# Expert weights of a hybrid block: loads of 1 MB into twelve slots become loads of 2 MB into six pairs of slots

## The chip, the cores and the metric

The kernel runs on one core of one Trainium2 chip. The metric is the device time of one execution in microseconds (us); before the change it was 2168.43 us, the median of three runs from 2166.55 to 2171.65.

## What is computed

One layer of a block over 512 tokens of width 1024, all in float32. Three token mixers (differential attention, mLSTM, cross-attention to 256 memory tokens) are computed side by side, gated, mixed and added to the input. Then follows the sparse part, which this case is about:

```
h = h + mix @ w_out
n = rms_norm(h)
top_v, top_i = top_k(n @ router_w + router_b, 4)          # 4 of 32 experts for each token
g, u = split(n @ w_gate_up[e] + b_gate_up[e])             # 1024 -> 2 x 1024
a = (clip(u, -7, 7) + 1) * min(g, 7) * sigmoid(1.702 * min(g, 7))
h = h + sum over the 4 experts of share * (a @ w_down[e] + b_down[e])
```

Each expert has 1024 x 2048 weights up and 1024 x 1024 down, 12 MB. All 32 are used, so 384 MB of weights pass through the core once.

## The kernel before

The program runs the mixers first, then the mix and the router, and near 1076 us the expert stage begins (`stage_moe`, from line 2178). The experts are taken in an order of their token counts that the router works out; every other one is "small" (at most 64 tokens).

The 12 MB of an expert are cut into 12 units of 1 MB: 128 partitions by 2048 floats, so that a partition's row of a unit is 8 KB. Units 0 to 3 and 8 to 11 are gate and up weights, units 4 to 7 (`DOWN`) the down weights. Each unit number has one slot in SBUF, `moe_raw[pos]`, at a place where an earlier stage kept something else. Four pairs of neighbouring slots lie in `xnH`/`xnL` (0 to 3) and `mixH`/`mixT` (4 to 7), the others in `y_caT` (8, 9) and `yH` (10, 11). Each slot has its own semaphore `s_moew[pos]`.

A unit goes through four engines. SyncE loads it (`load`, line 2233). ScalarE rounds it to its high part in `moe_hi`, a ring of six tiles (`hi`, line 2238). VectorE subtracts the high part from the raw one and leaves the low part in the slot itself (`lo`, line 2254). TensorE multiplies with both (`unit`, line 2262), 12 products of 128x512 for an ordinary expert, 8 for a small one, and counts the unit as used in `s_use`. ScalarE's rounding of a unit comes five units ahead of TensorE and waits for the unit's load and for the high tile that TensorE gave back six units earlier. VectorE is four units ahead.

TensorE's order in the loop is units 0 to 3 of expert n, units 4 to 7 of expert n-1, then units 8 to 11 of expert n, with the transposes of activations between. At the end (`LAST`) the down units of the last expert come in the order 6, 7, 4, 5. SyncE's list in the expert stage (`refill`, line 2525) is in order of position: wait until the slot's unit has been used, then load the same position of the next expert. After position 3 of the first expert it waits for the residual h with the down bias added, and stores h to the output (line 2535, 2 MB); ScalarE (line 2690) and GpSimd wait for this store before they go on to the second expert, since results are added onto the output in memory.

GpSimd gathers each expert's token rows from memory by an indirect DMA (`fetch`, line 2481) and scatters its results onto the output (`late`, line 2505); the first gather is issued in the router stage (line 1990). Before the expert stage, SyncE loads units 0 to 3 of the first expert early (line 1728) and, when the output projection is done, units 8 to 11 and 4 to 7 (line 1736). A barrier stands between the router stage and the expert stage (line 136).

Of the kernel before, what the change touches and what calls it, by code (L numbers as in the profile page):

```python
# [1601 lines left out]
def stage_mix(K, ctx):  # L1602
# [93 lines left out]
    def _(sp):  # L1696
# [24 lines left out]
        for dst, name in ((braw[0:NE, :], "b_gu"), (braw[NE:2 * NE, :], "b_gu"), (gf[:], "g_ffn"), (rw[:], "rw"),  # L1721
# [4 lines left out]
            sp.dma_start(dst, A[name]).then_inc(s_c, 16)  # L1726
        for u in range(4):
            sp.dma_start(K.moe_raw[u][:], A["w_moe"][u]).then_inc(K.s_moew[u], 16)
        sp.dma_start(K.lists.rearrange("(p r) f -> p (r f)", p=P), A["fill"]).then_inc(K.s_fill, 16)
        sp.dma_start(K.over, A["ove"]).then_inc(K.s_fill, 16)  # L1730
        for t in range(TT):
            sp.wait_ge(s_hn, t + 1)
            sp.dma_start(K.hn_d[t * P:(t + 1) * P, :], hn[:, t, :]).then_inc(s_hd, 16)
        for u in (8, 9, 10, 11, 4, 5, 6, 7):
            sp.wait_ge(s_o, 2 * TT)
            sp.dma_start(K.moe_raw[u][:], A["w_moe"][u]).then_inc(K.s_moew[u], 16)

# [153 lines left out]
    def _(act):  # L1891
# [57 lines left out]
        def moe_hi(u):  # L1949
            act.wait_ge(K.s_moew[u], 16)  # L1950
            act.wait_ge(s_o, TT)
            nc.scalar.activation(K.moe_hi[u][:], K.moe_raw[u][:], ACT.Copy).then_inc(s_mhi, 1)
# [226 lines left out]
def stage_moe(K, ctx):  # L2179
# [3 lines left out]
    HF, U = FF // 2, 4 * (FF // 2)  # L2183
    RAW, LO, HI, s_w, s_LG, s_Xg = K.moe_raw, K.moe_lo, K.moe_hi, K.s_moew, K.s_LG, K.s_Xg
    b0, b1 = K.base[K.xcT.name] + 4 * 2 * U, K.base[K.yH.name] + 4 * KT * S
# [47 lines left out]
    def load(sp, e, pos):  # L2233

        sp.dma_start(RAW[pos][:], A["w_moe"][ds(e * 12 + pos, 1)].rearrange("o p n -> (o p) n")
                     ).then_inc(s_w[pos], 16)

    def hi(act, n, pos):

        if not exists(n, pos):  # L2240
            return
        act.wait_ge(s_w[pos], n * 16 if pos in DOWN else n * 16 + 16)
        if isinstance(n, int) and n == 0:
            if pos in (10, 11):
                act.wait_ge(s_use, count(0, pos - 8))
        elif isinstance(n, int) and n == 1 and pos in (2, 3):
            act.wait_ge(s_use, count(0, pos + 8))
        elif isinstance(n, int) and n == NE:
            act.wait_ge(s_use, count(n - 1, pos if pos >= 6 else pos + 6))
        else:  # L2250
            act.wait_ge(s_use, count(n, pos - 6) if pos >= 6 else count(n - 1, pos + 6))
        nc.scalar.activation(HI[ring(n, pos)][:], RAW[pos][:], ACT.Copy).then_inc(s_hi, 1)  # L2252
# [269 lines left out]
    with nc.Block(no_gpsimd_drain=True) as block:  # L2522
        @block.sync
        def _(sp):
            def refill(n, first=False):

                here, ahead = None if first else expert(sp, n), expert(sp, n + 1)
                for pos in range(12):
                    if first and pos in DOWN:
                        continue  # L2530
                    sp.wait_ge(s_use, count(n, pos))
                    load(sp, here if pos in DOWN else ahead, pos)
                    if first and pos == 3:
                        sp.wait_ge(s_h1, 2 * TT)
                        sp.dma_start(A["out"].rearrange("(t p) d -> p t d", p=P), h1).then_inc(K.s_acc, 16)

            refill(0, True)
            with sp.Fori(1, NE - 1) as n:
                refill(n)
            here = expert(sp, NE - 1)  # L2540
            for pos in DOWN:
                sp.wait_ge(s_use, count(NE - 1, pos))
                load(sp, here, pos)

            def item(i, n):
                e = sp.value_load(K.over_sb[0:1, ds(i * 2, 1)], min_val=0, max_val=NE - 1)
                sp.wait_ge(s_use, i * 12 + B)
                for pos in ORDER:
                    load(sp, e, pos)
            overflow(sp, item, lambda: sp.wait_ge(K.s_ov, 20 * 16))  # L2550
            sp.wait_ge(s_sc, 16 * NE)
# [83 lines left out]
        def _(act):  # L2635
# [72 lines left out]
            def item(i, n):  # L2708
                base = i * 12 + B

                def item_hi(q):
                    pos = ORDER[q]
                    act.wait_ge(s_w[pos], n * 16 + 16)
                    act.wait_ge(s_use, base + (q - 5 if q >= 6 else 0))
# [147 lines left out]
def program(nc, A):  # L2862
    with ExitStack() as ctx:
# [17 lines left out]
        with ExitStack() as c0:  # L2881
# [9 lines left out]
            with ExitStack() as c1:  # L2891
                K.memH, K.memL = (K.sb(n, [P, KT, M], R32, ctx=c1) for n in ("memH", "memL"))
                with ExitStack() as c2:
# [28 lines left out]
                    [K.base[K.y_caT.name] + 4 * U * j for j in range(2)] + [K.base[K.yH.name] + 4 * U * j for j in range(2)]  # L2922
            K.moe_raw = [K.place(f"moe_raw{j}", U, at) for j, at in enumerate(homes)]
            K.moe_lo = [K.rounded(f"moe_lo{j}", K.moe_raw[j]) for j in range(12)]
            homes = [K.base[wraw.name] + 4 * U * j for j in range(4)] + [K.base[K.xcT.name] + 4 * U * j for j in range(2)]
            K.moe_hi = [K.place(f"moe_hi{j}", U, at, R32) for j, at in enumerate(homes)]
            K.moe_Xg = K.place("moe_Xg", D, K.base[K.sg[0].name])
            K.s_moew = [nc.alloc_semaphore(f"moe_unit{j}") for j in range(12)]
            K.s_acc, K.s_fill, K.s_ov, K.s_LG, K.s_Xg = (nc.alloc_semaphore(n) for n in (
# [7 lines left out]
def layouts(x, mem, attn_norm_g, w_in, b_gate, da_q_norm_g, da_k_norm_g, da_lambda_q1, da_lambda_k1,  # L2937
# [88 lines left out]
    for i, w in enumerate(units):  # L3026
        moe[:, i] = w.transpose(0, 1, 3, 2, 4)
    out["w_moe"] = moe.reshape(NE * 12, P, 4 * HF)
    out["b_gu"] = np.asarray(b_gate_up)[0].reshape(NE, 2, 2, HF).transpose(0, 2, 1, 3).reshape(NE, 2 * FF)
# [22 lines left out]
```

## Time and profile before

| | |
|---|---|
| median of three runs | 2168.43 us |
| profiled execution: span from first to last instruction | 2168.4 us (the profile gives no other time of its own) |
| TensorE products busy | 2111.0 us, 97% of the span |
| VectorE busy | 1564.6 us, 72% |
| ScalarE busy | 1318.4 us, 61% |
| GpSimd busy | 566.5 us, 26% |
| expert weight loads | 384 of 1024 KB, median 8.4 us from issue to landing |
| memory traffic in the expert stage | 383 to 405 GB/s in the profile's slices |

TensorE's busy time is an average over stages, and a busy TensorE is not one at its peak. In the slices of the expert stage TensorE, VectorE and the DMA engines all read nine tenths or more, so their shares alone do not say which of them sets the pace; the waits do. The rows further below are of the views that show them.

### The profile page before, as it was taken

The numbers are of one execution on the slowest core, as the hardware profiler recorded it, in microseconds if no ns is written. First come the engines' busy times: TensorE is split into PE (matmuls) and PEld (weight loads), VectorE is DVE, ScalarE is ACT, GpSimd is POOL, SyncE is SP. The second block draws the span as 40 slices with busy tenths as digits, with TensorE's granted clock in tenths as the row PEclk, the third lists the DMA queues.
The fourth block names the chain that finished last, engine by engine and source line by source line (L and its number), as shares of the span: only waits on it lengthen the run. The fifth ranks groups of instructions, "written<-read, shape, count | busy, mean of one in ns | idle before, by whom it ended". The sixth has DMA issues, their size and how long they took to land.

```text
span 2168.4 us, 29886 instructions
## 1 busy us (share of the span) xinstructions
PE 2111.0 (97%) x9638; PEld 1652.6 (76%) x9638; DVE 1564.6 (72%) x1690; ACT 1318.4 (61%) x1606; POOL 566.5 (26%) x429
## 2 busy tenths in 40 slices
PE   6999899999999999999899999999999999999998
PEld 6888677776667888888767777777777777777776
DVE  6777454754444334434689999999999999999996
ACT  5566453334232433323468888888888888888884
POOL 3333100201232000000214234443244332343421
PEclk9999999999999999999799999999999999999999
DMA  5110232320112343435589999999999999999993
GB/s 193 59 58 29 98 117 78 133 78 30 49 40 88 97 136 97 136 96 165 204 325 376 405 391 391 405 391 401 392 391 399 397 385 402 388 393 399 393 395 120
DMA packets 87095, 516.01 MB, mean 238 GB/s; under 512 B 13124, under 2 KB 14148, under 8 KB 36264
## 3 DMA queue, kind: packets, MB, share of 16 engines
q1 hardware_dynamic: 79448, 498.30, 59.6%
q0 software_dynamic: 7296, 16.79, 3.2%
q8 instruction: 37, 0.61, 0.1%
q14 instruction: 26, 0.21, 0.0%
q10 hardware_dynamic: 288, 0.09, 0.0%
HBM read 504.91 MB, written 19.40 MB: 242 GB/s over the span
## 4 chain that ended last, share of the span: by engine, by line
PE 49%; DVE 1%; DMA 0%; ACT 0%; issue 0%; POOL 0%; POOLq 0%; DVEq 0%; ACTq 0%
PE bank L2276 9%; PE bank L2278 8%; PE bank L2277 8%; PE bank L2269 8%; PE bank L2270 8%; PE bank L2311 3%; PE bank L2298 1%; PE bank L2287 1%; PE bank L2360 1%; DVE moe_lo L2259 1%; DMA out<-y_daT 0%; PE bank L2347 0%; DVE y_daT L2336 0%; ACT moe_hi L2252 0%; PE bank L2352 0%
## 5 line engine op out<-in xcount | busy, mean ns | idle before, releaser
L2259 DVE TENSOR_TENSOR moe_lo<-moe_raw,moe_hi 128x2048 fp32r<-128x2048 f32 x382 | 857.1, 2286 | 7.1 <-ACT moe_hi L2252 5.4
L2252 ACT ACTIVATE moe_hi<-moe_raw 128x2048 fp32r<-128x2048 f32 x380 | 722.3, 1915 | 62.8 <-PE bank L2278 54.4
L173 ACT ACTIVATE unit_hi<-unit_raw 128x1024 fp32r<-128x1024 f32 x116 | 122.2, 1059 | 241.8 <-DMA unit_raw<-in_w_units 235.7
L179 DVE TENSOR_TENSOR unit_lo<-unit_raw,unit_hi 128x1024 fp32r<-128x1024 f32 x116 | 145.3, 1258 | 163.5 <-ACT unit_hi L173 163.1
L2276 PE MATMUL bank<-moe_hi,moe_XTh 128*128 128x512 f32 x540 | 215.9, 400 | 0.0
L2278 PE MATMUL bank<-moe_hi,moe_XTl 128*128 128x512 f32 x540 | 211.5, 392 | 0.0
L2277 PE MATMUL bank<-moe_lo,moe_XTh 128*128 128x512 f32 x540 | 211.0, 391 | 0.0
L2269 PE MATMUL bank<-moe_hi,moe_XTh 128*128 128x512 f32 x480 | 194.5, 405 | 2.8 <-DVE moe_lo L2259 2.8
L2270 PE MATMUL bank<-moe_lo,moe_XTh 128*128 128x512 f32 x480 | 190.8, 398 | 0.0
L2503 POOL TENSOR_SCALAR moe_y<-moe_y,moe_LS 64x512 f32<-64x512 f32 x15 | 93.2, 6213 | 324.3 <-ACT moe_y L2466 324.3
L2505 POOL DMA_INDIRECT out<-moe_y,moe_LS x32 | 117.8, 3680 | 229.5 <-ACT moe_y L2466 215.9
L2276 PEld LDWEIGHTS bank<-moe_hi,moe_XTh 128*128 128x128 f32 x540 | 101.6, 188 | 43.6 <-issue 24.3
L2269 PEld LDWEIGHTS bank<-moe_hi,moe_XTh 128*128 128x128 f32 x480 | 91.2, 190 | 46.5 <-DVE moe_lo L2259 14.9
L2278 PEld LDWEIGHTS bank<-moe_hi,moe_XTl 128*128 128x128 f32 x540 | 101.3, 188 | 22.6
L2277 PEld LDWEIGHTS bank<-moe_lo,moe_XTh 128*128 128x128 f32 x540 | 101.5, 188 | 20.8
L2276 PE MATMUL bank<-moe_hi,moe_aTh 128*128 128x512 f32 x272 | 107.8, 396 | 0.6 <-DVE moe_lo L2259 0.6
L2270 PEld LDWEIGHTS bank<-moe_lo,moe_XTh 128*128 128x128 f32 x480 | 91.1, 190 | 20.5
L2278 PE MATMUL bank<-moe_hi,moe_aTl 128*128 128x512 f32 x272 | 106.1, 390 | 0.0
L2277 PE MATMUL bank<-moe_lo,moe_aTh 128*128 128x512 f32 x272 | 105.9, 389 | 0.0
L1749 PE MATMUL bank<-yH,unit_hi 128*128 128x512 f32 x256 | 100.4, 392 | 2.0 <-DVE mix_da_lo L1640 2.0
L1751 PE MATMUL bank<-yH,unit_lo 128*128 128x512 f32 x256 | 100.5, 393 | 0.0
L393 PE MATMUL bank<-da_slab_hi,xnH 128*128 128x384 f32 x256 | 92.3, 361 | 5.3 <-DVE xnL L214 5.3
(411 smaller groups left out, 4486.1 us busy)
## 6 DMA issues: line engine op xcount, KB each, us to landing
moe_raw<-in_w_moe SPq DMA_DIRECT2D x384, 1024.0 KB, 8.4
unit_raw<-in_w_units SPq DMA_DIRECT2D x116, 512.0 KB, 3.6
da_slab<-in_w_qkv SPq DMA_DIRECT2D x8, 1536.0 KB, 6.8
y_caT<-in_x SPq DMA_DIRECT2D x4, 512.0 KB, 5.8
yda_d<-y_daT SPq DMA_DIRECT2D x1, 2048.0 KB, 6.3
y_daT<-in_blocks_qk SPq DMA_DIRECT2D x1, 2048.0 KB, 10.9
y_daT<-yda_d SPq DMA_DIRECT2D x1, 2048.0 KB, 7.9
y_daT<-in_x SPq DMA_DIRECT2D x1, 2048.0 KB, 8.6
```

Of the source, the lines that this page charges most:

```text
L173: K.nc.scalar.activation(K.whi[:, i, :], K.wraw[:, i, :], ACT.Copy).then_inc(K.s_whi, 1)
L179: K.nc.vector.tensor_tensor(K.wlo[:, i, :], K.wraw[:, i, :], K.whi[:, i, :].bitcast(F32), ALU.subtract).then_inc(K.s_wlo, 1)
L1749: nc.tensor.matmul(bank[:], whi[:, i, w], hi[:, x], start=(k0 + k == 0), stop=False)
L1751: mm = nc.tensor.matmul(bank[:], wl, hi[:, x], start=False, stop=(k0 + k == depth - 1))
L2252: nc.scalar.activation(HI[ring(n, pos)][:], RAW[pos][:], ACT.Copy).then_inc(s_hi, 1)
L2259: nc.vector.tensor_tensor(LO[pos][:], RAW[pos][:], HI[ring(n, pos)][:].bitcast(F32), ALU.subtract).then_inc(s_lo, 1)
L2269: nc.tensor.matmul(bank[:], xh[:, x], HI[ring][:, w], start=start and k == 0, stop=False)
L2270: mm = nc.tensor.matmul(bank[:], xh[:, x], LO[pos][:, w], start=False, stop=stop and k == 3)
L2276: nc.tensor.matmul(bank[:], xh[:, x], HI[ring][:, w], start=start and k == 0, stop=False)
L2277: nc.tensor.matmul(bank[:], xh[:, x], LO[pos][:, w], start=False, stop=False)
L2278: mm = nc.tensor.matmul(bank[:], xl[:, x], HI[ring][:, w], start=False, stop=stop and k == 3)
L2505: nc.gpsimd.indirect_dma_start(A["out"], bass.IndirectOffsetOnAxis(ap=LS[0:rows, 0:1], axis=0), y[0:rows, :], None, bounds_check=S - 1, oo ...
```

## The change

The slots become six tiles of 2 MB, `moe_two[j]`, each over two neighbouring slots; the twelve `moe_raw` and `moe_lo` are views into them, at the same places as before. The weights lie in memory so that a partition's rows of two neighbouring units are one row of 16 KB. One DMA loads a pair, and there is one semaphore for each pair. SyncE waits for the use of the odd slot of a pair and then loads both. ScalarE waits for the pair's semaphore before it rounds either unit. The overflow path (experts with more than 128 tokens, not entered in this run) is changed in the same way.

```diff
-        for u in range(4):
-            sp.dma_start(K.moe_raw[u][:], A["w_moe"][u]).then_inc(K.s_moew[u], 16)
+        for u in range(2):
+            sp.dma_start(K.moe_two[u][:], A["w_moe"][u]).then_inc(K.s_moew[u], 16)
...
-        for u in (8, 9, 10, 11, 4, 5, 6, 7):
+        for u in (4, 5, 2, 3):
             sp.wait_ge(s_o, 2 * TT)
-            sp.dma_start(K.moe_raw[u][:], A["w_moe"][u]).then_inc(K.s_moew[u], 16)
+            sp.dma_start(K.moe_two[u][:], A["w_moe"][u]).then_inc(K.s_moew[u], 16)
...
     def load(sp, e, pos):
-        sp.dma_start(RAW[pos][:], A["w_moe"][ds(e * 12 + pos, 1)].rearrange("o p n -> (o p) n")
-                     ).then_inc(s_w[pos], 16)
+        sp.dma_start(TWO[pos // 2][:], A["w_moe"][ds(e * 6 + pos // 2, 1)].rearrange("o p n -> (o p) n")
+                     ).then_inc(s_w[pos // 2], 16)
...
     def hi(act, n, pos):
-        act.wait_ge(s_w[pos], n * 16 if pos in DOWN else n * 16 + 16)
+        act.wait_ge(s_w[pos // 2], n * 16 if pos in DOWN else n * 16 + 16)
...
             def refill(n, first=False):
-                for pos in range(12):
+                for pos in range(1, 12, 2):
                     if first and pos in DOWN:
                         continue
                     sp.wait_ge(s_use, count(n, pos))
                     load(sp, here if pos in DOWN else ahead, pos)
...
-            for pos in DOWN:
+            for pos in DOWN[1::2]:
                 sp.wait_ge(s_use, count(NE - 1, pos))
                 load(sp, here, pos)
...
-            K.moe_raw = [K.place(f"moe_raw{j}", U, at) for j, at in enumerate(homes)]
-            K.moe_lo = [K.rounded(f"moe_lo{j}", K.moe_raw[j]) for j in range(12)]
+            K.moe_two = [K.place(f"moe_two{j}", 2 * U, at) for j, at in enumerate(homes[0::2])]
+            K.moe_raw = [K.moe_two[j // 2][:, j % 2 * U:(j % 2 + 1) * U] for j in range(12)]
+            K.moe_lo = [K.rounded(f"moe_lo{j}", K.moe_two[j // 2], U, j % 2 * U) for j in range(12)]
...
-    out["w_moe"] = moe.reshape(NE * 12, P, 4 * HF)
+    out["w_moe"] = moe.reshape(NE * 6, 2, P, 4 * HF).transpose(0, 2, 1, 3).reshape(NE * 6, P, 8 * HF)
```

## Rows read from the trace of the kernel before

**Rows 1.** The page, busy time of TensorE over the span.

```profile
PE 2111.0 (97%) x9638; PEld 1652.6 (76%) x9638; DVE 1564.6 (72%) x1690; ACT 1318.4 (61%) x1606; POOL 566.5 (26%) x429
```

**Rows 2.** Engine shares by stretch: PE, PEld, DVE, ACT, POOL busy, clock, DMA share, GB/s.

```profile
1060.00:1070.00 10.00, 9.28 (x54) 9.04 (x55) 8.49 (x35) 0.00 (x0) 3.78 (x4) 0.50 1.01 424
1110.00:1120.00 10.00, 6.83 (x21) 5.22 (x22) 9.97 (x7) 10.00 (x9) 2.97 (x2) 0.77 0.97 394
1300.00:1400.00 100.00, 100.00 (x437) 75.38 (x436) 96.28 (x63) 82.92 (x69) 44.52 (x18) 1.00 1.01 396
```

**Rows 3.** Waits from 1140 (SyncE: 1100) us on: total, times, longest.

```profile
POOL moe_LS L2471 <- DMA out<-moe_y,moe_LS: 29.8, 15, 2.2
...
SPq L2235 <- PE bank L2278: 487.9, 187, 13.6
```

**Rows 4.** Chain of waits, token transposes of two experts apart: start, duration, what.

```profile
1142.66 0.88 PE bank L2287 x8
...
1209.08 0.87 PE bank L2287 x8
```

**Rows 5.** Expert weight loads issued from 1142 to 1209 us.

```profile
L2235 SPq DMA_DIRECT2D moe_raw<-in_w_moe x24: 332/333/336, 1142.8 to 1207.4; - x24
...
DMA to landing us min/median/max: 6.5/8.5/9.9
```

**Rows 6.** The four loads issued from 1084 to 1096 us.

```profile
L2235 SPq DMA_DIRECT2D moe_raw<-in_w_moe x4: 333/338/348, 1084.6 to 1094.6; - x4
...
DMA to landing us min/median/max: 4.7/4.8/5.1
```

**Rows 7.** The load of y_daT from its scratch copy (line 1168), 2 MB.

```profile
DMA to landing us min/median/max: 7.9/7.9/7.9
```

**Rows 8.** The load issued at 1162.0 us, and ScalarE's timeline at slot 2's rounding.

```profile
L2235 SPq DMA_DIRECT2D moe_raw<-in_w_moe x1: 333/333/333, 1162.0 to 1162.0; - x1
...
DMA to landing us min/median/max: 6.9/6.9/6.9
...
1174.10 1.91 ACT L2252 ACTIVATE moe_hi<-moe_raw 128x2048 fp32r<-128x2048 f32 x1
```

**Rows 9.** First gather, the next gather's landing (1079.3 us), and TensorE's start.

```profile
L1990 POOL DMA_INDIRECT moe_Xg<-hn_d,first x1: 1295/1295/1295, 1064.9 to 1064.9; - x1
...
DMA to landing us min/median/max: 8.8/8.8/8.8
...
DMA to landing us min/median/max: 3.6/3.6/3.6
...
1075.73 1.94 PE L2287 MATMUL bank<-ident,moe_Xg 128*128 128x128 f32 x8 [3.20 <-PEq L136]
```

**Rows 10.** The second of the four loads of rows 6.

```profile
L2235 SPq DMA_DIRECT2D moe_raw<-in_w_moe x1: 342/342/342, 1087.9 to 1087.9; - x1
```

**Rows 11.** Chain of waits at the store of h and where TensorE goes on.

```profile
1096.18 9.16 DMA out<-y_daT
...
1118.72 1.09 PE bank L2360 x4
```

**Rows 12.** Last four loads; ScalarE's, the chain's and VectorE's rows at the end.

```profile
L2235 SPq DMA_DIRECT2D moe_raw<-in_w_moe x4: 332/332/333, 2128.1 to 2136.3; - x4
...
2138.37 1.92 ACT L2252 ACTIVATE moe_hi<-moe_raw 128x2048 fp32r<-128x2048 f32 x1 [1.07 <-DMA moe_raw<-in_w_moe]
...
2142.39 0.60 ACT L2409 ACTIVATE moe_sg<-bank 128x512 f32<-128x512 f32 x1 [2.11 <-PE bank L2278]
...
2148.23 0.70 DVE moe_um L2417
...
2149.56 2.29 DVE L2259 TENSOR_TENSOR moe_lo<-moe_raw,moe_hi 128x2048 fp32r<-128x2048 f32 x1
```

**Rows 13.** GpSimd's copy after a scatter landed, and ScalarE's write to the buffer.

```profile
1192.88 2.23 POOL L2471 COPY moe_LS<-first 128x4 int32 x1
...
1199.35 0.69 ACT L2466 ACTIVATE moe_y<-bank,moe_LS 128x512 f32<-128x512 f32 x1 [2.12 <-PE bank L2278]
```

More of the change, by code:

```diff
@@ L1949, in moe_hi @@
         def moe_hi(u):
-            act.wait_ge(K.s_moew[u], 16)
+            act.wait_ge(K.s_moew[u // 2], 16)
             act.wait_ge(s_o, TT)
@@ L2183, in stage_moe @@
     HF, U = FF // 2, 4 * (FF // 2)
-    RAW, LO, HI, s_w, s_LG, s_Xg = K.moe_raw, K.moe_lo, K.moe_hi, K.s_moew, K.s_LG, K.s_Xg
+    RAW, TWO, LO, HI, s_w, s_LG, s_Xg = K.moe_raw, K.moe_two, K.moe_lo, K.moe_hi, K.s_moew, K.s_LG, K.s_Xg
     b0, b1 = K.base[K.xcT.name] + 4 * 2 * U, K.base[K.yH.name] + 4 * KT * S
@@ L2547, in item @@
                 sp.wait_ge(s_use, i * 12 + B)
-                for pos in ORDER:
+                for pos in ORDER[0::2]:
                     load(sp, e, pos)
@@ L2712, in item_hi @@
                     pos = ORDER[q]
-                    act.wait_ge(s_w[pos], n * 16 + 16)
+                    act.wait_ge(s_w[pos // 2], n * 16 + 16)
                     act.wait_ge(s_use, base + (q - 5 if q >= 6 else 0))
@@ L2927, in program @@
             K.moe_Xg = K.place("moe_Xg", D, K.base[K.sg[0].name])
-            K.s_moew = [nc.alloc_semaphore(f"moe_unit{j}") for j in range(12)]
+            K.s_moew = [nc.alloc_semaphore(f"moe_two{j}") for j in range(6)]
             K.s_acc, K.s_fill, K.s_ov, K.s_LG, K.s_Xg = (nc.alloc_semaphore(n) for n in (
```

## The prediction

> **What bounds the kernel now.** I read the page first, then the engine shares by stretch, the waits, the chain of waits and last the loads themselves. TensorE is busy 2111.0 of 2168.4 us [rows 1]. The expert stage begins near 1076 us; in a stretch of it TensorE is busy 100.00 of 100 us at clock 1.00, VectorE 96, ScalarE 83, and the DMA share is 1.01 at 396 GB/s [rows 2]. Two resources look full, so the question is which of them the others wait for. Between 1140 and 2100 us no wait of a compute engine on an expert weight load is listed; the only DMA in the list is the output scatter, 29.8 us on GpSimd, at most 2.2 each. SyncE's queue, in contrast, waits 487.9 us on one TensorE line alone before it may issue a load [rows 3]. So the loads are held back by TensorE and not the reverse. Two experts take 1209.08 - 1142.66 = 66.4 us [rows 4], fixed by TensorE; in that time 24 loads of 1 MB go out, one per 2.77 us, and land 6.5 to 9.9 us after issue, median 8.5 [rows 5]. A load issued when little is in flight needs 4.7 to 5.1 us [rows 6]. There is a queue, then, but it does not grow into a stall.
>
> The profiled span equals the median of the runs shown to 0.1 us (2168.4 and 2168.43), so the sum is made on 2168.4.
>
> **What changes.** In the loop 24 issues per two experts become 12 of 2 MB. The bytes are the same. The even slot of a pair is asked for one unit later than now, when its odd neighbour has been used, and both halves count as landed only when 2 MB have landed. Nothing is added on TensorE, VectorE or ScalarE; their waits go to six semaphores instead of twelve. SyncE issues half as often, which is worth nothing, as it is idle behind TensorE [rows 3].
>
> **A pair alone.** No pair of this tensor is in the trace. From below: 4.8 us for 1 MB [rows 6] plus another 1 MB at the 424 GB/s of the eight queued loads [rows 2], 2.5 us, is 7.3 us. From above: the one load of 128 rows of 16 KB at a quiet time, y_daT back from its scratch copy, took 7.9 us [rows 7]. I take 7.3 where the rest of the case is like [rows 6], and keep 7.9.
>
> **The steady stage: 0.** The tightest place found is the pair of slots 2 and 3. Its refill would be issued at 1162.0 us, when slot 3 is free. The single load issued there landed after 6.9 us, that is 2.1 over one alone, so 2.1 us stood in front of it. ScalarE splits slot 2 again from 1174.10 us [rows 8]. The pair would land at 1162.0 + 7.3 (7.9) + 2.1 = 1171.4 (1172.0), 2.1 to 2.7 us ahead of need. At the longest latency of [rows 5], 9.9 us, the queue in front is 5.1 us and a pair lands after 12.4 to 13.0 us; if that met this place, where 1174.10 - 1162.0 = 12.1 us are left, it would be 0.3 to 0.9 us late. Behind it there is a second cover: ScalarE idles 17% and splits a unit five units ahead of TensorE. If this cover goes, the price is rival A. A gain is excluded as well: TensorE has nothing to win where no wait on a load is listed. Ends: -1 and +1 us by small shifts, A apart.
>
> The Trainium skill, page "SBUF — State Buffer", section "The DMA setup-cost knee", says that each DMA pays about 2 us that don't scale with its bytes, and advises the largest single transfer. By that rule half the issues would win time. The trace agrees for one load alone but not for a queue: 424 GB/s with eight 1 MB loads queued leaves no room for 2 us each. As an estimate by that page the 2 us saved would be hidden in this stage in any case.
>
> **The first gather: +0.6 us.** The rows of the first expert's tokens are gathered by a GpSimd DMA at 1064.9 us while the eight loads issued before it are still running (424 GB/s [rows 2]); it lands after 8.8 us, at 1073.7. The next gather, at 1079.3 with the queue nearly empty, lands after 3.6 us. TensorE turns the tokens at 1075.73, released by the barrier between the stages and not by the gather [rows 9]. So the load in front costs a gather 5.2 us now, and there are 2.0 us of cover. Doubled rows make it wait behind doubled packets at most: +5.2 us, which would put the start 3.2 us later. At least nothing changes, as the bytes in front are the same. Of the range of the landing, 0 to +5.2, I take the middle, +2.6: 0.6 us beyond the cover. Ends 0 and +3.2.
>
> The Trainium skill, page "DMA: Bandwidth & Descriptors", section "Queues, rings and completion order", has each DMA engine take turns between queues by whole packets, which speaks against larger rows wherever a small transfer shares the engines. By that rule the gather is later, as above; without it this term is 0 and the sum 0.6 less.
>
> **The store of h before the second expert: +2.3 us.** After the first expert's slots 0 to 3 are used, four loads go out (1084.6 to 1094.6 [rows 6], the second at 1087.9 [rows 10]), then the 2 MB store of h to the output. It is issued at 1096.18 and lands 9.16 us later, at 1105.34, and the chain runs through it: ScalarE waits for it, then VectorE, and TensorE goes on at 1118.72 [rows 11]. Now the last load ahead of it lands at 1094.6 + 5.1 = 1099.7 and the store 5.6 us after that. With pairs, slots 0 and 1 come at 1087.9 and land by 1095.8 at the latest; slots 2 and 3 come at 1094.6, not earlier, and land at 1101.9 to 1102.5. The store follows 5.6 us later, at 1107.5 to 1108.1: +2.2 to +2.8. The megabyte asked for at 1091.4 until now has to move in front of the store instead. All of ScalarE's and VectorE's work behind is in order and busy (VectorE 9.97 of 10 us at 1110 to 1120 [rows 2]), so the delay goes through to TensorE. I take +2.3. If the engines do not serve in order of issue the store hides part: lower end +0.5.
>
> TensorE's clock is 0.77 in that same stretch [rows 2], after TensorE stood idle before it. A longer idle time may move or lengthen the low stretch (1.2 instead of 2.4 GHz). A stretch like this one costs about 2.3 us of full-speed work; as part of it falls where TensorE waits anyway, I take 0 and keep -1.5 and +2.
>
> **The last refills: +2.2 us.** The last four loads go out from 2128.1 to 2136.3, and at the very end slots 6 and 7 are used before 4 and 5. Slot 6, the last but one, is split at 2138.37, after ScalarE waited 1.07 us for its landing; this is the only such wait in the last 60 us. With pairs, 6 and 7 come together at 2136.3, land at 2143.6 (2144.2), and the split of 6 starts there, 5.2 us later. ScalarE works in order: split 6 (1.92), the activation it now runs at 2142.39 (0.60, of which 0.1 overlaps), split 7 (1.92), which ends 4.35 us on, at 2148.0. VectorE then needs 2.29 for the low part of 7, twice 0.70 for the two steps of the activation and 2.29 for the low part of 4: 2153.9 to 2154.0. In the trace that last part runs from 2149.56 for 2.29 us, to 2151.85, and TensorE takes slot 4 when it ends [rows 12]. So +2.0, or +2.6 with 7.9; I take +2.2. Ends: +1.5, and +3.5 if the pair also queues behind that of 4 and 5. The final scatter comes after all loads and doesn't change.
>
> **The scatter inside the loop: 0.** Where least time is left a scatter has landed by 1192.88 us, GpSimd then copies the next list for 2.23 us, and ScalarE needs both at 1199.35 [rows 13]: it can be 4.2 us later. If it lost 5.2 us, like the gather at its upper end, ScalarE would be 1.0 us late per two experts, inside its idle 17%.
>
> **Sum.** 0.6 + 2.3 + 2.2 = +5.1 us; 2168.4 + 5.1 = 2173.5 us. Own range of this case: 2170.5 to 2177.5.
>
> **Rivals.**
> A. The DMA engines become the bound, far slower. The share is 1.01 already [rows 2], and a pair that is asked for later can leave them idle, or 16 KB rows may move worse beside the scatter. It decides from the point at which 2 MB cost more than 66.4 / 12 = 5.53 us of the engines, everything else included. If they cost 5.6, the 7.9 us of [rows 7] less the 2.3 that 1 MB alone has over 2.5, two experts take 0.8 us longer and the 15 rounds of two 12 us: 2173.5 + 12 = about 2185. Against it: [rows 5] shows latency far from its limit, and in bytes per time a queue of large rows has no reason in the trace to be worse. Chance 0.16.
> B. The end terms are partly hidden, because transfers already in flight overlap and the store passes the last pair: 0.5 at the store, 1.5 at the end, 0 at the gather, so 2170.4. Chance 0.20.
> C. It gets faster: larger rows in fewer transfers empty the queue sooner. At most that gives back what waits for such transfers: the 1.07 us at the end [rows 12], and of the store's 9.16 us the 3.5 beyond the 5.6 that it takes behind a load [rows 11]. Both together, 4.6: 2163.8. No row speaks for it, and the pair's later issue works against it at both places. The rule of "SBUF — State Buffer" in the Trainium skill, above, points this way. Chance 0.08.
>
> **How the numbers follow.** The forecast has 0.56, the rivals 0.16, 0.20 and 0.08. A measurement of this kernel tells 0.2%, 4.3 us, from no change. The forecast, +5.1, lies just above this: some 0.38 of its 0.56 are slower, 0.18 same. With A that is 0.54 slower; B and 0.02 of C add up to 0.40 same; 0.06 faster. The range leaves out the lower part of C and the upper part of A: 2166.5 to 2184.
>
> **What would show it.** Right: still no wait on weight loads between 1140 and 2100 us and two experts in 66.4 us; pairs landing in 9 to 13 us there and in 7.3 to 7.9 us alone; ScalarE released by the store some 11.5 us after its issue; at the end a wait of about 5 to 6 us on the load instead of 1.07. Wrong: waits of ScalarE or VectorE on the loads in the loop with TensorE below 100 (A); two experts taking less than 66.4 us (C, or something not seen here); the store landing 9.2 us after issue (B).

## The result and the profile after

The changed kernel takes 2177.78 us, the median of four runs (2176.66 to 2179.62), against 2167.49 us for the kernel before in the same comparison: ratio 1.0047, 95% interval 1.0032 to 1.0061, or +10.2 us (+6.9 to +13.2). Timed again later (e0, below) it came out at ratio 1.0036 (1.0023 to 1.0049), +7.8 us. It is slower by about twice the +5.1 us of the forecast. The time lies inside the forecast's range and just outside the likeliest case's own range (2170.5 to 2177.5).

The profiled execution after has a span of 2178.0 us (its own time 2179.62). First the page: busy times of the engines, and the loads with their size and median time to landing.

```profile
PE 2112.9 (97%) x9638; PEld 1654.5 (76%) x9638; DVE 1564.9 (72%) x1690; ACT 1318.1 (61%) x1606; POOL 599.4 (28%) x429
...
moe_two<-in_w_moe SPq DMA_DIRECT2D x192, 2048.0 KB, 11.0
```

TensorE's work is unchanged [rows 1]. There are half as many loads, each landing after 11.0 us in the median, where the single ones took 8.5 [rows 5]. GpSimd's busy time rose by 33 us, which has no weight at 28%. Next the engine shares by stretch (columns as in [rows 2]), and the waits from 1145 to 2110 us (for SyncE from 1100 us on).

```profile
1300.00:1400.00 100.00, 100.00 (x438) 75.68 (x437) 96.29 (x64) 85.03 (x70) 44.76 (x18) 1.00 1.00 397
```

```profile
POOL moe_LS L2471 <- DMA out<-moe_y,moe_LS: 88.2, 29, 5.1
...
SPq L2235 <- PE bank L2278: 543.3, 94, 16.4
```

The loop is as it was: TensorE 100.00 of 100 us, 397 GB/s. Still no wait of a compute engine on a weight load is listed there, and SyncE still waits for TensorE. What grew is GpSimd's wait for its scatters, 29.8 to 88.2 us and 5.1 at most against 2.2 [rows 3]. It costs nothing, as no such wait stands in the chain of waits (start, duration, what). This is the kernel after:

```profile
1068.42 11.09 DMA moe_Xg<-hn_d,first
1079.55 1.98 PE bank L2287 x8
...
1099.41 12.40 DMA out<-y_daT
...
1125.18 0.66 PE bank L2360 x4
...
1147.53 0.87 PE bank L2287 x8
...
2111.38 0.87 PE bank L2287 x8
...
2141.15 10.17 DMA moe_two<-in_w_moe
2151.34 1.92 ACT moe_hi L2252
2153.28 2.32 DVE moe_lo L2259 x2
...
2157.77 0.69 DVE moe_um L2417
...
2159.18 2.21 DVE moe_lo L2259
2161.44 0.50 PE bank L2276
...
2171.58 1.51 POOL out L2505
```

And these are the rows of the kernel before that answer to its last part; its chain has no DMA in that part:

```profile
2106.50 0.87 PE bank L2287 x8
...
2149.65 2.21 DVE moe_lo L2259
2151.90 0.50 PE bank L2276
...
2162.04 1.51 POOL out L2505
```

Three anchors stand in every chain: TensorE's first transposes of the stage (x8), those of the second expert at 1141 to 1148 us, and those of the last expert. They cut the time into a start, a loop and an end:

| | before | after | difference |
|---|---|---|---|
| stage begins | 1075.73 | 1079.55 | +3.8 |
| start: to the second anchor | 66.93 | 67.98 | +1.0 |
| loop: to the third anchor | 963.84 | 963.85 | 0.0 |
| end: to the last row | 55.54 | 60.20 | +4.7 |

The loop of 964 us did not move. The end grew by 4.7 us, all of it by 2161.44: from there to the last row it is 10.14 us in both. In the start the store of h takes 12.40 us instead of 9.16 [rows 11], but from its landing to the second anchor it is 35.72 us against 37.32. This and the +3.8 before the stage are looked at with the table of all profiles.

### The profile page after: what moved, and what is told of

Same layout as the page of the kernel before. It is cut to its first block, busy times and chain, and to the rows that moved or that the text cites. A ratio compares the mean times of both kernels' runs of the same rounds, so it can differ in the third digit from the quotient of the medians.

```text
span 2178.0 us, 29142 instructions
## 1 busy us (share of the span) xinstructions
PE 2112.9 (97%) x9638; PEld 1654.5 (76%) x9638; DVE 1564.9 (72%) x1690; ACT 1318.1 (61%) x1606; POOL 599.4 (28%) x429
## 3 DMA queue, kind: packets, MB, share of 16 engines
q1 hardware_dynamic: 51800, 498.29, 59.3%
## 4 chain that ended last, share of the span: by engine, by line
PE 82%; DMA 3%; DVE 1%; ACT 1%; issue 0%; POOL 0%; SPq 0%; POOLq 0%; ACTq 0%; DVEq 0%
PE bank L2276 9%; PE bank L2278 8%; PE bank L2277 8%; PE bank L2269 8%; PE bank L2270 8%; PE bank L1749 5%; PE bank L1750 5%; PE bank L1751 5%; PE bank L2311 3%; PE bank L1184 2%; PE bank L1186 2%; PE bank L1185 2%; PE bank L1278 2%; PE bank L1249 2%; PE bank L2298 1%; PE bank L2287 1%
## 5 line engine op out<-in xcount | busy, mean ns | idle before, releaser
L2259 DVE TENSOR_TENSOR moe_lo<-moe_two,moe_hi 128x2048 fp32r<-128x2048 f32 x382 | 857.0, 2286 | 13.0 <-ACT moe_hi L2252 11.3
L2252 ACT ACTIVATE moe_hi<-moe_two 128x2048 fp32r<-128x2048 f32 x380 | 721.9, 1914 | 69.2 <-PE bank L2278 52.6
```

Source lines behind the costliest of these rows:

```text
L2259: nc.vector.tensor_tensor(LO[pos][:], RAW[pos][:], HI[ring(n, pos)][:].bitcast(F32), ALU.subtract).then_inc(s_lo, 1)
```

## The experiments

The theory after this reading: the loop costs nothing, and the whole loss lies at the two places where something waits for a load directly, the store of h in the first refill and the last refills. The rivals are that the longer rows cost time, that it is the bytes' new place in memory, and that the part before the stage (+3.8) is systematic (U).

### e0, the changed kernel again

No edit.

> The changed kernel once more, for a tighter ratio and a second profile. Between the two profiles so far the span grew by 9.6 us: 3.5 before the expert stage begins, where no instruction differs, 0.3 at the first gather, 3.2 at the store of h, 4.7 at the last refills, and -2.2 in between by the clock. Theory T (three places at the start and the end of the expert stage; the loop gives 0): +6 to +9 us over the kernel before, and the expert stage begins anywhere between 1075 and 1080 us, as in the kernel before. Rival U (something ahead of the stage is really later, by the weights' new place in memory or the program's length): +10 us or more, and the stage begins at 1079 us or later each time.

Measured: 2178.11 us against 2170.35, ratio 1.0036 (1.0023 to 1.0049), +7.8 us, inside theory T's +6 to +9. The stage begins at 1077.55, the store takes 12.37 us, and the load at the end is in the chain again. The chain of e0 at the end:

```profile
2111.35 0.87 PE bank L2287 x8
...
2141.12 9.05 DMA moe_two<-in_w_moe
...
2160.30 0.50 PE bank L2276
...
2161.91 0.43 PE bank L2278
...
2172.02 1.51 POOL out L2505
```

The last products begin 1.1 us earlier than in the first profile, yet the end is 60.67 us, longer than 60.20. Eight products run at 0.41 to 0.43 us instead of 0.23, and from 2160.30 to the last row it is 11.72 us against 10.14. The granted clock of that stretch:

```profile
2160.00:2165.00 5.00, 4.70 (x14) 3.75 (x15) 3.04 (x3) 0.00 (x0) 0.00 (x0) 0.66 0.00 2
```

It is 0.66, so most of it is at 1.2 instead of 2.4 GHz. TensorE had stood idle three times in the 8 us before: 1.5 us before the unit of slot 6, 0.5 us before the transposes, and 1.54 us before its last unit. In the first profile its idle times were 2.64 and 0.83 us, and the low stretch came earlier, during the unit of slot 6. The clock of that stretch, and TensorE's timeline at the start of the unit of slot 6 and of the last one:

```profile
2155.00:2159.00 4.00, 3.28 (x8) 2.63 (x9) 3.96 (x4) 4.00 (x3) 0.00 (x0) 0.57 0.00 0
...
2155.72 0.77 PE L2276 MATMUL bank<-moe_hi,moe_aTh 128*128 128x512 f32 x1 [2.64 <-DVE moe_lo L2259]
...
2161.44 0.50 PE L2276 MATMUL bank<-moe_hi,moe_aTh 128*128 128x512 f32 x1 [0.83 <-DVE moe_lo L2259]
```

There the slow products only shortened TensorE's next wait for VectorE, so they cost nothing on the path. In the kernel before the clock is 1.00 from 2142 to 2151 us and from 2155 to 2159 us, around its last units. So the late pair costs twice: ScalarE's wait itself, and in some executions 1.4 to 1.6 us for the clock after it.

### e1, pairs of 2 MB in rows of 8 KB

The memory layout of before; a load takes two units and has 256 rows of 8 KB.

```diff
...
-        sp.dma_start(TWO[pos // 2][:], A["w_moe"][ds(e * 6 + pos // 2, 1)].rearrange("o p n -> (o p) n")
+        sp.dma_start(TWO[pos // 2][:].rearrange("p (u n) -> p u n", u=2),
+                     A["w_moe"][ds(e * 12 + pos // 2 * 2, 2)].rearrange("u p n -> p u n")
...
```

> Pairs of slots refilled by one DMA of 2 MB, but the weights lie in memory as before the change, so the DMA has 256 rows of 8 KB. Theory T with the pairing as the cause: a pair alone still lands after 7.3 to 8.1 us, the store of h after 11 to 12.4 us, the wait at the last refills is 7 to 9 us; time as the changed kernel within 1.5 us. Rival R (the 16 KB rows themselves move worse, which is why a pair alone took 8.1 us and the last one 10.2 instead of 7.3): a pair alone lands after about 7.2 us, the last one after 7.5 to 8.5, the store after 11.0, and the time is 2.5 to 4 us below the changed kernel.

Measured: 2175.76 us, ratio 1.0031 (1.0020 to 1.0042), +6.7 us. The store takes 12.59 us and the last load is in the chain as before:

```profile
1094.57 12.59 DMA out<-y_daT
...
2136.50 8.87 DMA moe_two<-in_w_moe
```

The pairing makes most of the loss, not the row length. The last load takes 8.87 us here and 9.05 in e0, and the end, 58.90 us, differs from e0's 60.67 by the clock (1.6 us; here it stays at 1.00) and this 0.2. The timing alone can't decide it: the median is 2.4 us below e0's, between theory T's 1.5 and rival R's 2.5 to 4, and the two intervals overlap widely. Among the transfers only the small ones tell the rows apart. Between 1145 and 2100 us the median gather lands after 13.1 us in the changed kernel, 10.3 here and 10.0 before; the median scatter after 14.7, 12.4 and 11.6. Longer rows hold up a small transfer beside them by 2 to 3 us, but in the loop every such transfer has cover. The first gather lands after 9.0 us here, against 11.1 in the changed kernel and 8.8 before.

### e2, single loads out of 16 KB rows

The layout of the changed kernel, the loads and slots of the kernel before.

```diff
...
-        sp.dma_start(RAW[pos][:], A["w_moe"][ds(e * 12 + pos, 1)].rearrange("o p n -> (o p) n")
+        sp.dma_start(RAW[pos][:], A["w_moe"][ds(e * 6 + pos // 2, 1), :, pos % 2 * U:(pos % 2 + 1) * U].rearrange("o p n -> (o p) n")
...
```

> The reverse: the weights lie in memory in rows of 16 KB as after the change, but each slot is loaded by its own DMA of 1 MB (half of each row) as soon as it is free, with its own semaphore. Theory T: as the kernel before within 1 us, the store lands after 9.2 us, a single alone after 4.8. Rival R (the layout in memory costs): 2 to 4 us over the kernel before, singles alone over 5.2 us. Rival U (weights' place in memory delays what comes ahead): the stage begins at 1079 us or later.

Measured: 2170.49 us, ratio 1.0002 (0.9993 to 1.0011). The store takes 9.31 us, the median gather 10.0, the end 55.54. The new place of the bytes in memory costs no time that shows. One of rival R's signs is there all the same: the single loads ahead of the store take 5.3 us in the median, not 4.8, but nothing waits for them.

### e5, pairs in the loop, single loads at both ends

Slots 0 to 3 in the first refill and slots 4 to 7 in the last are loaded singly, each even slot on a semaphore of its own.

```diff
...
+                if first:
+                    for pos in range(4):
+                        sp.wait_ge(s_use, count(0, pos))
+                        load_half(sp, ahead, pos)
...
-            for pos in DOWN[1::2]:
+            for pos in DOWN:
                 sp.wait_ge(s_use, count(NE - 1, pos))
-                load(sp, here, pos)
+                load_half(sp, here, pos)
...
```

> The changed kernel with pairs everywhere but at two places: the four refills ahead of the store of h (slots 0 to 3) and the last four (4 to 7) are again loads of 1 MB, each issued when its slot is free. The loop keeps its pairs. Theory T: the store lands after 9.2 us and the last wait is about 1.1 us, so 3.2 + 4.7 = 7.9 us come back; +0 to +1.5 us over the kernel before is left (the gather's 0.3 and noise). Rival L (the loop with pairs costs too, hidden in the first comparison by the clock): +3 us or more over the kernel before. Rival U: +3 us or more, with the stage's begin at 1079 us or later.

Measured: 2170.08 us, ratio 0.9998 (0.9989 to 1.0007). Store 9.06 us, end 55.54 us. With pairs in all of the loop and in the early loads nothing is lost beyond the 1.5 us that the interval leaves, and nothing clear is won either. So rival L falls, and the cost sits in those eight megabytes.

### e3 and e4, single loads at one end only

e3 has the first half of the diff of e5, e4 the second.

> The changed kernel, with loads of 1 MB again only for slots 0 to 3 ahead of the store of h. In the first comparison the store's landing cost 3.2 us (12.4 against 9.2) and the last refills 4.7. Theory T: the store lands after 9.2 us, the last wait stays at 8 to 9 us; the time lies 3 us below the changed kernel and about 4.5 to 5 us over the kernel before. Rival M (the two places are not additive, one hides behind the other through the clock): under 1.5 or over 5 us below the changed kernel.

> The changed kernel, with loads of 1 MB again only for the last four refills (slots 4 to 7 of the last expert). Theory T: the last wait on a load falls from 8 or 9 us to between 1 and 3; the store of h still lands after 12.4 us; the time lies 4.5 to 5 us below the changed kernel, about 3 us over the kernel before. Rival M: under 3 or over 6.5 us below the changed kernel.

Measured: e3 2175.53 us, ratio 1.0034 (1.0021 to 1.0047), +7.4 us; e4 2171.33 us, ratio 1.0014 (1.0005 to 1.0023), +3.0 us. The chain of e3, where only the end is paired:

```profile
1096.50 9.39 DMA out<-y_daT
...
2106.83 0.87 PE bank L2296 x8
...
2136.59 10.12 DMA moe_two<-in_w_moe
...
2168.40 1.51 POOL out L2514
```

The chain of e4, where only the start is:

```profile
1095.65 12.22 DMA out<-y_daT
...
2107.43 0.87 PE bank L2296 x8
...
2162.97 1.51 POOL out L2514
```

Each place has its own mark, and undoing one leaves the other. e4's end is 55.54 us to the digit of the kernel before; e3's is 61.57, with slow products like e0's. The two differences add up to 10.4 us, against the 10.2 and 7.8 of the whole change. So the end is the larger part, as in the profiles. But e3 lies only 0.4 us below e0 (2.8 below the first comparison), where 3 us was expected: that meets rival M's sign, under 1.5 us. With five executions of e3 and an interval of +4.6 to +10.2 us the timing doesn't decide it. In its profile the store lands after 9.39 us again, as expected, but the last pair takes 10.12 us and the end is the longest of all. e4 met its expectation; ScalarE waits 1.8 us in all for its last loads.

### e6, the store of h ahead of the pair of slots 2 and 3

```diff
                     sp.wait_ge(s_use, count(n, pos))
-                    load(sp, here if pos in DOWN else ahead, pos)
                     if first and pos == 3:
                         sp.wait_ge(s_h1, 2 * TT)
                         sp.dma_start(A["out"].rearrange("(t p) d -> p t d", p=P), h1).then_inc(K.s_acc, 16)
+                    load(sp, here if pos in DOWN else ahead, pos)
```

> The changed kernel with the store of h issued ahead of the pair of slots 2 and 3 instead of behind it. Theory T (the store's 12.4 us are its place behind a pair that could not be asked for earlier): the store lands after 6 to 7 us, so ScalarE goes on 5 to 6 us earlier; the pair of slots 2 and 3 then lands some 13 us after the store's issue, which ScalarE meets 8 us after it goes on, hence a new wait of 0 to 2 us. Time 4 to 5.5 us below the changed kernel. Rival O (the store waits for memory or for writes, not for the pair): it still lands after 10 us or more and the time is within 1.5 us of the changed kernel.

Measured: 2171.75 us, ratio 1.0013 (1.0004 to 1.0022), +2.8 us, with all loads still pairs. One of its twelve executions took 7400.68 us; the ratio is made without it. The waits of ScalarE from 1060 to 1150 us:

```profile
ACT moe_XTh L2387 <- DMA out<-y_daT: 7.4, 1, 7.4
```

The store lands after 7.55 us, and ScalarE waits 7.4 us for it, against 12.16 in the changed kernel. The pair behind the store lands 12.0 us after its issue and is not late: no wait on a load is listed in the start. By the ratios this is 5 us below e0, as theory T had it, though the store took 7.55 us and not 6 to 7; rival O falls.

### e8, the same move in the kernel before

The store goes ahead of the loads of slots 2 and 3; the loads are single.

```diff
-                    sp.wait_ge(s_use, count(n, pos))
-                    load(sp, here if pos in DOWN else ahead, pos)
-                    if first and pos == 3:
+                    if first and pos == 2:
                         sp.wait_ge(s_h1, 2 * TT)
                         sp.dma_start(A["out"].rearrange("(t p) d -> p t d", p=P), h1).then_inc(K.s_acc, 16)
+                    sp.wait_ge(s_use, count(n, pos))
+                    load(sp, here if pos in DOWN else ahead, pos)
```

> The kernel before the change, with the store of h issued ahead of the loads of slots 2 and 3. Theory T: the store lands after 6.3 us instead of 9.2, issued at the same time; the loads of slots 2 and 3 come 5 and 2 us later and land some 2 us before ScalarE needs them; 2 to 3 us below the kernel before. Rival O: the store still lands after 9 us and the time is unchanged within 1 us, or the later loads make ScalarE wait and it is 1 us slower.

Measured: 2167.32 us against 2168.56, ratio 0.9995 (0.9986 to 1.0004). The store takes 7.63 us instead of 9.16 and the start is 65.20 instead of 66.93 us. Theory T expected the store after 6.3 us and a gain of 2 to 3 us. The store took longer than that, and the gain of the profile, 1.7 us, is below what this timing can tell.

### e9, which weights go into the pair that comes free first

The last-but-one expert gives back slots 4 and 5 first, but the last units are used in the order 6, 7, 4, 5. So the units needed first were loaded last. Here the last two loads change their contents: slots 4 and 5 take units 6 and 7, and ScalarE, VectorE and TensorE read them there (`slot_of` is `pos ^ 2` for the last round).

```diff
...
                 sp.wait_ge(s_use, count(NE - 1, pos))
-                load(sp, here, pos)
+                load(sp, here, pos, pos ^ 2)
...
```

> The changed kernel; in the last two loads the pair of slots that comes free first (4 and 5) takes the weights that are needed first (units 6 and 7 of the last expert), the other pair takes units 4 and 5. Same rows, same 2 MB, same order of use. Theory (the end costs what it does because the unit that is needed first sits in the pair that is asked for last, behind another pair): the first of the two pairs is issued at about 2135.7 and lands after 7.6 to 8.2 us, so ScalarE waits 1 to 2 us for it instead of 9.2; the second lands 8.7 to 10.2 us after 2141.1 and is waited for 1.5 to 3.5 us, which VectorE's work hides. The stretch from the last token transpose to the end goes from 60.2 back to 55.5 to 56.5 us, and the time is that of the changed kernel with single loads at the end: 2170.5 to 2172.5 against 2168.5 before, ratio 1.0010 to 1.0018. Rival (two pairs back to back are late whichever is needed first): the wait moves to the second pair, the stretch is 57 to 60 us, the time 2173.5 to 2176.5.

Measured: 2172.07 us against 2170.12, ratio 1.0010 (1.0001 to 1.0019), +2.2 us. ScalarE's timeline at the first of these units (start, duration, what, idle time before it and its releaser):

```profile
2140.38 1.91 ACT L2257 ACTIVATE moe_hi<-moe_two 128x2048 fp32r<-128x2048 f32 x1 [1.28 <-DMA moe_two<-in_w_moe]
```

The same row of the changed kernel:

```profile
2151.34 1.91 ACT L2252 ACTIVATE moe_hi<-moe_two 128x2048 fp32r<-128x2048 f32 x1 [9.15 <-DMA moe_two<-in_w_moe]
```

A wait of 9.15 us became one of 1.28, the second pair is not waited for at all, and the end is 55.54 us again. So the price at the end needs both, loads of 2 MB and this order: single loads in the old order (e4) and pairs in the new one (e9) have the same end, 55.54 us.

### e10 and e11, both moves together, with pairs and without

e10 is e9 with the edit of e6. e11 is e8 with the exchange of e9 in its four last single loads.

> As the one before, and the store of h goes out ahead of the pair of slots 2 and 3 in the first refill. All loads stay pairs of 2 MB. Theory (both costs are matters of order, not of size): from the stage's first transpose to the transpose of the first loop round 63.7 us, as with the store moved alone (66.9 before), the end 55.5 to 56.5 us; together 3 us less than the kernel before, 2164.5 to 2167, ratio 0.9980 to 0.9993. Rival (pairs cost some 2 us more at the start than those two stretches show, since the kernel with single loads at the end alone was timed 2.8 us above before while its profile showed 1.0): 2167 to 2169, ratio 0.9993 to 1.0003. Rival (the order at the end doesn't matter): 2171 to 2173.

> The kernel before, with single loads, the store of h ahead of the loads of slots 2 and 3, and in the last four loads the same exchange (slots 4 and 5 take units 6 and 7). It asks whether the 1.07 us that ScalarE waits for its last loads cost anything in the kernel before, and is what the paired version has to beat. Theory (the wait is off the path: in the chain TensorE runs through to VectorE's last steps): no wait on the last loads, the end still 55.5 us, the time that of the store moved alone, 2166.5 to 2168, ratio 0.9988 to 0.9998. Rival (the wait is on the path): the end 54.5 us, another 1.1 us less, 2165.5 to 2166.9.

Measured: e10 2169.15 us, ratio 0.9994 (0.9985 to 1.0003); e11 2169.33 us, ratio 0.9991 (0.9982 to 1.0000). The chain of e10:

```profile
1077.23 1.98 PE bank L2292 x8
...
1097.55 7.54 DMA out<-y_daT
...
1142.35 0.87 PE bank L2292 x8
2106.19 0.87 PE bank L2292 x8
...
2161.73 1.51 POOL out L2510
```

Start 65.12, loop 963.84, end 55.54 us. With all loads paired the kernel is level with the kernel before: the interval ends at +0.03%. The expected 3 us of gain did not come. The time is nearer to the first rival, 2167 to 2169, but its reason, a cost of pairs that the stretches don't show, is not what the profile has. e10's start is 65.12 and not e6's 63.71 because of the clock, as the next part shows: e6's profile was a lucky one to build the expectation on. e11 has no wait on its last loads and the same end of 55.54 us, so the 1.07 us that ScalarE waits there in the kernel before [rows 12] cost nothing. The two versions can't be told apart, and a gain over the kernel before is not established for either: at best it is e11's 2 us, with an interval that ends at 1.0000.

### The three stretches in all profiles

Worked out from each chain by its anchors, in us, each from one profiled execution; the ratio is that of the timed runs.

| kernel | stage begins | store of h | start | end | ratio |
|---|---|---|---|---|---|
| before | 1075.73 | 9.16 | 66.93 | 55.54 | 1 |
| after | 1079.55 | 12.40 | 67.98 | 60.20 | 1.0047 |
| e0 | 1077.55 | 12.37 | 69.96 | 60.67 | 1.0036 |
| e1 | 1074.48 | 12.59 | 68.41 | 58.90 | 1.0031 |
| e2 | 1075.98 | 9.31 | 66.63 | 55.54 | 1.0002 |
| e5 | 1076.96 | 9.06 | 66.09 | 55.54 | 0.9998 |
| e3 | 1076.19 | 9.39 | 66.80 | 61.57 | 1.0034 |
| e4 | 1075.72 | 12.22 | 67.87 | 55.54 | 1.0014 |
| e6 | 1078.70 | 7.55 | 63.71 | 61.47 | 1.0013 |
| e8 | 1076.09 | 7.63 | 65.20 | 55.54 | 0.9995 |
| e9 | 1076.69 | 12.23 | 67.77 | 55.54 | 1.0010 |
| e10 | 1077.23 | 7.54 | 65.12 | 55.54 | 0.9994 |
| e11 | 1080.62 | 7.57 | 64.83 | 55.54 | 0.9991 |

The loop is 963.84 or 963.85 us in all thirteen. The stage begins at 1075.73, 1076.09 and 1080.62 in before, e8 and e11, which are the same program up to there: U falls, the +3.8 us of the first comparison is scatter of this kind. The start varies by 1.5 to 2 us with the same code (67.98 and 69.96 in after and e0). With the store behind paired loads it is 68.4 on the mean of five profiles, with it behind single loads 66.6 of four, and with the store ahead of slots 2 and 3 64.7 of four. So the start costs about 1.8 us, of the 3.2 us by which the store lands later.

The traces show where the rest goes. From the store's landing to the point where TensorE goes on with the transposes (x4) it is 13.37 or 13.38 us in all thirteen profiles, so the whole delay arrives at TensorE. From there to the second anchor it is either 22.3 to 22.4 us or 23.7 to 23.9, and the granted clock of the first 6 us tells the two apart. Here are those 6 us in the kernel before and after, and in e6 and e10, whose code is the same up to there (columns as in [rows 2]):

```profile
1118.72:1124.72 6.00, 6.00 (x18) 4.12 (x19) 6.00 (x4) 4.19 (x6) 0.00 (x0) 0.72 0.40 142
...
1125.18:1131.18 6.00, 6.00 (x25) 4.10 (x26) 6.00 (x4) 5.77 (x6) 0.00 (x0) 1.00 0.72 303
...
1120.07:1126.07 6.00, 6.00 (x25) 4.10 (x26) 6.00 (x4) 5.77 (x6) 0.00 (x0) 1.00 0.99 423
...
1118.47:1124.47 6.00, 6.00 (x18) 3.54 (x19) 6.00 (x4) 4.22 (x6) 0.00 (x0) 0.72 1.00 429
```

At 1.00 the stretch is short (after, e1, e4, e9, e6), at 0.72 to 0.75 long (all others). Up to the point where TensorE goes on, the start is 42.85 us on the mean with single loads ahead of the store, 45.74 with pairs, and 41.2 with the store moved ahead, whether the loads are single or paired. So the pairs cost 2.9 us there, and the clock gave 1.5 us back in four of five profiles.

What stays open: start and end make 5.7 us of the difference in the first profile and 8.2 in e0's, 6.9 on the mean, and the timed differences are 10.2 and 7.8. The intervals reach down to that (the lower ends are 6.9 and 5.0), so nothing more is claimed. Why the clock falls at one time and not at another in the same code is open too.

## Why the forecast was right in kind and too small in size

**The steady stage, 0: right.** 963.85 against 963.84 us, no wait on a load. From 1145 to 2100 us the pairs land after 8.9 to 13.7 us, median 11.1, where 9 to 13 was expected. In the place that was held to be the tightest, the pair is issued at 1166.8 us and lands after 10.2, 2.0 us ahead of ScalarE's rounding at 1178.99; 2.1 to 2.7 had been worked out. e5 shows that pairs in the loop alone cost nothing that can be timed.

**A pair alone, 7.3 (7.9) us: the upper value.** The first pairs of the first refill land after 8.1, 7.6 and 7.7 us in after, e0 and e9, the first of the last two after 7.6 and 7.7 in e0 and e9. The sum over a single 1 MB load plus 2.5 us was 0.3 to 0.8 too low.

**First gather, +0.6: right within its ends.** It lands 11.09 us after issue, +2.3 of the +2.6 taken, and now releases TensorE in place of the barrier. Issue to first transpose is 11.13 against 10.83 us [rows 9]: +0.3. That the row length does it is shown by e1, where the barrier ends the wait as before.

**Store of h, +2.3: the landing was mis-sized, the cost came out about right, partly by luck.** I expected the release some 11.5 us after issue; it was 12.40, 12.37, 12.59, 12.22 and 12.23. The pair in front was taken as one alone (landed by 1101.9), but it was issued 6.6 us after its neighbour, while that was still in flight, and took 9.0 us instead of 7.3; in the changed kernel it was issued at 1097.8 and landed at 1106.8, and the store 5.0 us after that (5.6 had been taken). The whole delay reaches TensorE, as the forecast had it, and 2.9 us on the mean are left of it there. The forecast took the clock at 0 and kept -1.5 as an end: it was that end in four of five profiles, 1.5 us given back, as the 6 us windows above show, and 0 in e0. So the term is +1.8 us on the mean at the second anchor. A landing taken some 0.9 us too early and a clock term left at 0 nearly cancel in the +2.3. e4 alone, timed, gives +3.0 (+1.1 to +5.0) for start and gather together, beside the forecast's 2.9.

**Last refills, +2.2: this step failed in its size.** It measured +4.7 to +6.0 us (end 60.20 to 61.57; with 8 KB rows 58.90, +3.4); e3, where only this end is paired, timed +7.4 (+4.6 to +10.2). Two things were missing. First, the pair of 6 and 7 was priced as one alone, and "if the pair also queues behind that of 4 and 5" was left to the upper end, +3.5. It queues always: it is issued 5.4 us after that pair, which takes 7.6 us, and lands after 10.17, 9.05, 10.12 and 9.98 us in after, e0, e3 and e6. The forecast's own rule for the loop, what is left of the load in front plus the time alone, would have said so: with the measured 7.6 us it gives 2.2 + 7.6 = 9.8 us. In before's time (4.88 us less) after's pair lands at 2146.4 and not at 2143.6, and the 2.8 us between go nearly one for one into VectorE's last part: 2.0 + 2.8 = 4.8, beside the measured 4.7. The split of slot 6 then begins 9.15 us after ScalarE was free, where 5 to 6 was expected (the forecast's own terms, 1.07 + 5.2, give 6.3). Second, the clock: I asked whether a longer idle time lowers it at the store, but not here. It falls there in all four of these profiles; in the first one this is off the path, in e0 it costs 1.6 us, in e3 and e6 1.4, with the same 0.43 us products.

**The scatter in the loop, 0: right.** It lands later by 3.1 us in the median (14.7 against 11.6), GpSimd waits for it 88.2 instead of 29.8 us, and nothing follows from it [rows 13].

**The rivals.** A fell: 397 GB/s and an unmoved loop. B fell: the store did not pass the pair and landed later, not as before. C fell: no profile has a shorter stretch by pairs alone, and e11 shows that the 1.07 us at the end were not to be won. The rule of the Trainium skill that was weighed for C ("SBUF — State Buffer", "The DMA setup-cost knee") counts a fixed cost for every transfer. One after the other it is borne out: a transfer of 2 MB alone took 7.6 to 8.2 us against twice 4.8 for two of 1 MB. But nothing here waits for two loads one after the other, and in the loop's queue half as many transfers move the same 397 GB/s, against 396 [rows 2]. The rule weighed at the gather ("DMA: Bandwidth & Descriptors", "Queues, rings and completion order": turns between queues by whole packets) agrees with e1: the same 2 MB in rows of 8 KB let gathers and scatters land 2.8 and 2.3 us earlier. The page of the profile counts 51800 packets in the queue of the loads after and 79448 before, so a row of 16 KB is not split into packets of the old size.

## What to carry to other kernels

Before loads are made larger, look for the places where a load or a store is waited for directly, the first and the last of a stream and whatever stands in the same queue behind them: the loop had slack and hid the doubled size, and these few places carried all of the loss that the experiments could place. Price a large transfer there with its neighbour still in flight, not as one alone. And before giving up the larger transfer, check the order: putting the units needed first into the slots that come free first took 9.15 us of waiting down to 1.28, and moving one store ahead took 12.4 us down to 7.5, with all loads still 2 MB. That brought the kernel back to level and not below: no gain of 2 MB loads over 1 MB loads was measured here.

## What was not expected of the hardware

A second 2 MB load that is issued 5.4 to 6.6 us after one that lands in 7.6 to 8.1 us takes 8.6 to 10.2 us itself. That is roughly its time alone plus the 1.5 to 2.2 us that are left of the first. Single loads of 1 MB in the same places, 2.7 to 3.5 us apart, also had 1.2 to 2.1 us left of their neighbour in front, yet took 4.7 to 5.1 us, no more than the first of them ([rows 6]; 4.8 to 4.9 at the end). So overlap that was free for small loads was not free for large ones; why is not shown. Two 2 MB loads issued 5.4 us apart, the later of them landed 15.6 us after the first was issued, are 4 MB at some 270 GB/s with the time to land included, against 397 in the loop.

And the granted clock fell near the end in after, e0, e3 and e6, after TensorE had stood idle for 0.5 to 2.6 us at a time, and then products of 128x512 took 0.43 us instead of 0.23, six to eight of them in a row in e0, e3 and e6. In e1, with idle times of the same kind, it stayed at 1.00.
